# A two-layer encoder step on one core: five hand-overs between its stages rearranged, the differential map combined ahead of the next maxima, and the values of a step ahead of the second part of a weight block

## The reference

```python
hn = rms_norm(h, norm_mix_g)
z = hn @ w_in        # split into qa, ka, va, cq, dkv, ga, gb
oa = diff_attention(qa, k_all, v_all, q_pos, k_pos, lam, bias_table)   # 8 heads, two maps each
oa = rms_norm(oa, a_subln_g) * (1.0 - lam_init) @ w_a_br
ob = mla_attention(...) @ w_b_br                                       # 8 heads, latent keys
m = sigmoid(ga) * oa + sigmoid(gb) * ob
h = h + m @ w_out
h = h + conv_ffn(rms_norm(h, norm_ffn_g))
```

## Time and profile before

| | |
|---|---|
| median of 3 runs | 3051.67 us (3051.27 to 3070.66) |
| profiled execution | 3043.57 us, of which the span of instructions is 3042.0 |
| PE busy | 2723.2 us, 90% of the span |
| PE weight loads | 2505.8 us, 82% (they overlap the products) |
| DVE, ACT, POOL busy | 1467.0, 941.2, 252.0 us |
| mean granted TensorE clock | 0.939 of full speed |
| differential loops | 614.5 to 814.4 and 2100.0 to 2299.6 us |

### The profile page before, as it was taken

How to read it: one execution, slowest core, us unless ns; L and a number is a source line. 1 busy time by engine, 2 the same in 40 slices (tenths; PEclk the granted TensorE clock), 3 DMA queues, 4 the chain that set the end, 5 groups by cost and what they waited for, 6 DMA issues and landing times.

```text
span 3042.0 us, 53054 instructions
## 1 busy us (share of the span) xinstructions
PE 2723.2 (90%) x17464; PEld 2505.8 (82%) x17464; DVE 1467.0 (48%) x2602; ACT 941.2 (31%) x2032; POOL 252.0 (8%) x684
## 2 busy tenths in 40 slices
PE   5898989789889899999988889997997999999996
PEld 5875879667689899999978568885776988999996
DVE  5635221244444674655657342213445347646375
ACT  3324223345421331322233332233453113323122
POOL 3100100110000010100001011011000001001010
PEclk8979989889999999999989899998999999999998
DMA  4220114411122222222123002234111222222222
GB/s 124 52 60 0 51 44 124 149 44 42 39 62 63 67 69 73 73 69 74 58 65 70 27 8 64 68 116 134 42 39 42 76 63 66 69 73 73 69 69 75
DMA packets 376797, 201.32 MB, mean 66 GB/s; under 512 B 66438, under 2 KB 368636, under 8 KB 376658
## 3 DMA queue, kind: packets, MB, share of 16 engines
q1 hardware_dynamic: 346722, 178.99, 21.0%
q10 hardware_dynamic: 25344, 12.27, 1.3%
q0 software_dynamic: 4592, 8.35, 0.9%
HBM read 183.84 MB, written 17.88 MB: 66 GB/s over the span
## 4 chain that ended last, share of the span: by engine, by line
PE 77%; DVE 6%; issue 6%; ACT 4%; DVEq 3%; DMA 2%; ACTq 1%; SPq 0%; POOL 0%; POOLq 0%
PE ps L547 21%; PE ps L551 20%; PE ps L548 20%; PE ps L687 1%; PE ps L644 1%; PE ps L714 1%; DVE rstd L1638 1%; DMA k_past<-in_cache_a_k 1%; ACT w_hi L1171 1%; PE ps L586 1%; PE ps L589 1%; PE ps L617 1%; PE ps L712 1%; DVEq L1749 1%; PE tp L702 1%
## 5 line engine op out<-in xcount | busy, mean ns | idle before, releaser
L547 PE MATMUL ps<-hn_hi,w_hi 128*128 128x328 f32 x2848 | 893.0, 320 | 13.7 <-DVE ob_lo L1937 7.7
L548 PE MATMUL ps<-hn_lo,w_hi 128*128 128x328 f32 x2848 | 878.3, 314 | 0.0
L551 PE MATMUL ps<-hn_hi,w_lo 128*128 128x328 f32 x2848 | 662.8, 315 | 0.0
L1620 DVE TENSOR_TENSOR w_lo<-w_raw,w_hi 128x1024 fp32r<-128x1024 f32 x300 | 366.9, 1223 | 511.4 <-ACT w_hi L1171 505.6
L1171 ACT ACTIVATE w_hi<-w_raw 128x1024 fp32r<-128x1024 f32 x300 | 316.7, 1057 | 849.0 <-PE ps L551 627.6
L547 PEld LDWEIGHTS ps<-hn_hi,w_hi 128*128 128x128 f32 x2848 | 539.1, 189 | 34.7 <-issue 29.8
L548 PEld LDWEIGHTS ps<-hn_lo,w_hi 128*128 128x128 f32 x2848 | 539.7, 190 | 0.2
L551 PEld LDWEIGHTS ps<-hn_hi,w_lo 128*128 128x128 f32 x2848 | 485.8, 189 | 0.0
L547 PE MATMUL ps<-s_hi,w_hi 128*128 128x328 f32 x704 | 220.7, 320 | 18.5 <-DVE w_lo L1620 14.0
L548 PE MATMUL ps<-s_lo,w_hi 128*128 128x328 f32 x704 | 220.3, 318 | 0.0
L551 PE MATMUL ps<-s_hi,w_lo 128*128 128x328 f32 x704 | 166.9, 320 | 0.0
(11 more groups left out here) (333 smaller groups left out, 4130.7 us busy)
## 6 DMA issues: line engine op xcount, KB each, us to landing
w_raw<-in_w_in SPq DMA_DIRECT2D x98, 512.0 KB
w_raw<-in_w_up SPq DMA_DIRECT2D x88, 512.0 KB
w_raw<-in_w_down SPq DMA_DIRECT2D x32, 512.0 KB
out<-tok_out ACTq DMA_DIRECT2D x32, 256.0 KB, 2.3
k_past<-in_cache_a_k SPq DMA_DIRECT2D x16, 512.0 KB, 5.0
v_past<-in_cache_a_v SPq DMA_DIRECT2D x16, 512.0 KB, 3.5
w_raw<-in_w_a_br SPq DMA_DIRECT2D x16, 512.0 KB
w_raw<-in_w_out SPq DMA_DIRECT2D x16, 512.0 KB
```

The lines of the kernel that those rows point to most:

```text
L547: mm(dst[:, c, :], w_hi[:, slot, k, :], x_hi[:, k, cols], start=(k == 0), stop=False)
L548: mm(dst[:, c, :], w_hi[:, slot, k, :], x_lo[:, k, cols], start=False, stop=False)
L551: last = mm(dst[:, c, :], w_lo[:, slot, k, :], x_hi[:, k, cols], start=False, stop=(k == nk - 1))
L1620: tt(w_lo[:, slot], w_raw[:, slot], w_hi[:, slot].bitcast(F32), ALU.subtract).then_inc(w_split[slot], 1)
```

## The change

Nothing is computed differently. In the order of the layer:

- Latent outputs: the eight products of the first key block stand between the eight heads' small products, ahead of the wait for ob_done.
- Decode part: SP loads the keys of stream n+3 ahead of the values of stream n, where it was n+2.
- Before the differential loop: POOL waits only for the last decode scores and the map of the last stream but one, stages the first two heads and starts their bias loads, and then loads v_meta. PE waits for v_meta in the first `values` of two heads. In SBUF d_eT and d_bias change places, so that what is staged early lies on buffers that are free by then.
- In the loop: PE runs values(u) ahead of the second part of the block; DVE runs finish(u) and the split ahead of maxima(u+1); ACT runs the gate's tanh ahead of the exponentials.
- Behind the loop: all four first gate blocks run before the wait for on_done, then four projections, then pairs as before. DVE's splits of blocks B_MA+2, +3 and +4 stand around its reciprocal, and a buffer gate_next holds the third and fourth gates.
- Output projection: the first block begins when six mixed tiles are ready, and waits for the seventh and eighth at its seventh and eighth products.

```diff
 o_sq, = run(names["par_rows"][0], ("o_sq", [P, 2, P]))
-ds_, d_bias, d_qs, d_eT, d_ks = run(
-    ZW, ("d_s", [P, 2, 2, PM]), ("d_bias", [P, 2, PM]), ("d_qs", [P, 2, SEQ]),
-    ("d_eT", [P, 2, QT + 1, P]), ("d_ks", [P, 2, PM]))
+ds_, d_eT, d_qs, d_bias, d_ks = run(
+    ZW, ("d_s", [P, 2, 2, PM]), ("d_eT", [P, 2, QT + 1, P]), ("d_qs", [P, 2, SEQ]),
+    ("d_bias", [P, 2, PM]), ("d_ks", [P, 2, PM]))
 o_stage, = run(names["d_qs"][0], ("o_stage", [P, 2, SEQ]))
...
 m_lo, = run(ZW, ("m_lo", [P, KD, T], F32R))
-gate, mixed = run(names["v_tok"][0], ("gate", [P, 2, T]), ("mixed", [P, 2, T]))
-assert names["mixed"][1] <= names["v_tok"][1]
+gate, mixed, gate_next = run(names["v_tok"][0], ("gate", [P, 2, T]), ("mixed", [P, 2, T]), ("gate_next", [P, 2, T]))
+assert names["gate_next"][1] <= names["v_tok"][1]
...
+        def first_a_block(t, n):
+            src = (w_in_v[l][:, :, COL_GA + t * P:COL_GA + (t + 1) * P], a_br_v[l][:, :, t * P:(t + 1) * P])[n]
+            load(l, B_MA + 4 * n + t, 0, KD, src)
         b_block(0, 0, 0)
...
         past_keys_after(3)
+        past_keys_after(4)
         for n in range(2, STREAMS):
-            if n + 2 < STREAMS:
-                past_keys_after(n + 2)
+            if n + 3 < STREAMS:
+                past_keys_after(n + 3)
             past_values(n)
...
                 b_block(i, *divmod(jn, 2))
-        with e.Fori(0, KD // 2) as i:
+        for n in range(2):
+            for t in range(4):
+                first_a_block(t, n)
+        with e.Fori(2, KD // 2) as i:
             for jn in range(4):
...
             step = l * H * QT + i2 * 2 * QT + u
+            if u == 0:
+                e.wait_ge(v_meta_loaded, l * 16 + 16)
             e.wait_ge(a["pT"], step + 1)
...
                     scores(*then)
+                values(i2, u)
                 mix_part(i2, u, 1)
-                values(i2, u)
...
+        slot = block_ready(l, B_K, 0)
         for h in range(H):
...
             last.then_inc(olat_mm, 1)
+            last = product(slot, h, KD, hn_hi, hn_lo)
+        last.then_inc(block_done[slot], 1)
...
-        for j in range(2):
-            project(l, B_K + j, 0, KD, hn_hi, hn_lo)
+        project(l, B_K + 1, 0, KD, hn_hi, hn_lo)
         tile_turned(0, 0)
...
         e.wait_ge(dn["out_done"], (l + 1) * OUTPUTS)
-        e.wait_ge(v_meta_loaded, l * 16 + 16)
         e.sem_inc(past_wait, 1)
...
                     outputs_turned(h)
+        for t in range(2, 4):
+            project(l, B_MA + t, 0, KD, hn_hi, hn_lo)
         e.wait_ge(on_done, l + 1)
...
-        for j in range(2):
-            project(l, B_MA + 2 + j, 0, KD, oa_hi, oa_lo)
-        with e.Fori(1, KD // 2) as i:
+        for t in range(4):
+            project(l, B_MA + 4 + t, 0, KD, oa_hi, oa_lo)
+        with e.Fori(2, KD // 2) as i:
             for n in range(2):
...
                     project(l, B_MA + 2 * n + j, i * 2, KD, *((hn_hi, hn_lo), (oa_hi, oa_lo))[n])
-        e.wait_ge(m_done, l * KD + KD)
-        e.sem_inc(past_wait, 1)
-        job(l, B_OUT, KD // 2, KD, m_hi, m_lo)
+        slot = block_ready(l, B_OUT, 0)
+        for k in range(KD):
+            if k == 0 or k >= KD - 2:
+                e.wait_ge(m_done, l * KD + max(k + 1, KD - 2))
+                e.sem_inc(past_wait, 1)
+            last = product(slot, k, KD, m_hi, m_lo)
+        last.then_inc(block_done[slot], 1)
+        project(l, B_OUT + 1, 0, KD, m_hi, m_lo)
+        job(l, B_OUT, KD // 2, KD, m_hi, m_lo, first=1)
...
             for u in range(2 * QT):
+                if u % 4 == 2:
+                    gate_b(i2, u // 4)
                 then = step_after(i2, u, 1, final)
...
                     exps(*then)
-                if u % 4 == 2:
-                    gate_b(i2, u // 4)
                 transposed(i2, u)
...
             s = arrived(l, B_MA + j, i * 2)
-            e.wait_ge(gate_used, l * KD if isinstance(i, int) else l * KD + t - 1)
+            e.wait_ge(gate_used, l * KD + t - 1)
             e.sem_inc(past_wait, 1)
...
+        def first_gate_a(t):
+            s = arrived(l, B_MA + t)
+            e.wait_ge(gate_used, l * KD)
+            e.sem_inc(past_wait, 1)
+            act(halves((gate, gate_next)[t // 2][:, t % 2]), accs(s), ACT.Tanh, scale=0.5).then_inc(acc_free[s], 1)
+            e.drain().then_inc(gate_ready, 1)
         for h in range(H):
...
             if h == 5:
-                gate_a(0, 0)
                 split(l, B_MA + 2)
+                first_gate_a(0)
+        split(l, B_MA + 3)
+        first_gate_a(1)
+        split(l, B_MA + 4)
+        first_gate_a(2)
         e.wait_ge(on_scaled, l + 1)
...
         act(oa_hi[:, :, 0:META], on_t[:, :, P:], ACT.Copy, scale=sub_gain).then_inc(on_hi_done, 1)
-        gate_a(0, 1)
-        split(l, B_MA + 3)
-        split(l, B_MA + 4)
-        with e.Fori(1, KD // 2) as i:
+        split(l, B_MA + 5)
+        first_gate_a(3)
+        for t in range(6, 9):
+            split(l, B_MA + t)
+        with e.Fori(2, KD // 2) as i:
             for n in range(4):
...
                 then = step_after(i2, u, 1, final)
-                if then:
-                    maxima(*then)
+                finish(i2, u)
                 if u % 2:
...
                     gated_b(i2, 0)
-                finish(i2, u)
                 e.drain()
+                if then:
+                    maxima(*then)
             gated_b(i2, 1)
...
         low_part(H - 1)
+        split(l, B_MA + 2)
         e.wait_ge(on_rms, l + 1)
...
         e.drain()
+        split(l, B_MA + 3)
         tt(on_t[:], oT_new[:], on_rstd[:], ALU.mult).then_inc(on_scaled, 1)
-        split(l, B_MA + 2)
+        split(l, B_MA + 4)
         e.wait_ge(on_hi_done, l + 1)
...
+        def gated(t, j, s, g, b, hi, lo):
+            e.wait_ge(gate_ready, l * (2 * KD) + t + (KD + 1))
+            e.sem_inc(past_wait, 1)
+            stt(halves(mixed[:, j]), halves(g), 1.0, accs(s), ALU.add, ALU.mult).then_inc(acc_free[s], 1)
+            e.drain().then_inc(gate_used, 1)
+            tt(mixed[:, j], mixed[:, j], b, ALU.add)
+            e.drain()
+            ts(hi, mixed[:, j], 0.5, None, ALU.mult)
+            e.drain()
+            stt(lo, mixed[:, j], 0.5, hi.bitcast(F32), ALU.mult, ALU.subtract).then_inc(m_done, 1)
         def mixed_tile(i, j):
             t = i * 2 + j
-            e.wait_ge(gate_ready, l * (2 * KD) + t + (KD + 1))
             s = arrived(l, B_MA + 2 + j, i * 2)
-            stt(halves(mixed[:, j]), halves(gate[:, j]), 1.0, accs(s), ALU.add, ALU.mult).then_inc(acc_free[s], 1)
-            e.drain().then_inc(gate_used, 1)
-            tt(mixed[:, j], mixed[:, j], one(mixed_b[:, ds(t, 1), :]), ALU.add)
-            e.drain()
-            ts(one(m_hi[:, ds(t, 1), :]), mixed[:, j], 0.5, None, ALU.mult)
-            e.drain()
-            stt(one(m_lo[:, ds(t, 1), :]), mixed[:, j], 0.5, one(m_hi[:, ds(t, 1), :]).bitcast(F32), ALU.mult, ALU.subtract).then_inc(m_done, 1)
-        for j in range(2):
-            split(l, B_MA + 3 + j)
-            mixed_tile(0, j)
-        with e.Fori(1, KD // 2) as i:
+            gated(t, j, s, gate[:, j], one(mixed_b[:, ds(t, 1), :]), one(m_hi[:, ds(t, 1), :]), one(m_lo[:, ds(t, 1), :]))
+        split(l, B_MA + 5)
+        for t in range(4):
+            if t < 3:
+                split(l, B_MA + 6 + t)
+            s = arrived(l, B_MA + 4 + t)
+            gated(t, t % 2, s, (gate, gate_next)[t // 2][:, t % 2], mixed_b[:, t], m_hi[:, t], m_lo[:, t])
+        with e.Fori(2, KD // 2) as i:
             for n in range(4):
...
-    def stage_heads(kind, l, rows, src, dst, biased):
+    def stage_heads(kind, l, rows, src, dst, biased, then=None):
...
         stage_pair(0, True)
+        if then:
+            then()
         with e.Fori(1, H // 2) as i2:
...
         staged_new(l * (STREAMS + 1) + STREAMS, slice(0, META), False)
-        e.wait_ge(dn["out_done"], (l + 1) * OUTPUTS)
-        for j in range(2):
-            e.wait_ge(tok_stored[j], l * (48 * KD) + 48 * KD)
+        e.wait_ge(dn["scores"], (l + 1) * (STREAMS + 1))
+        e.wait_ge(dn["pturned"], l * (STREAMS + 1) + STREAMS)
         e.sem_inc(past_wait, 1)
         e.drain()
-        e.dma_start(v_meta[:], a_v_prompt[l, 0, 0:META].rearrange("t h e -> t (h e)")).then_inc(v_meta_loaded, 16)
-        stage_heads("diff", l, slice(0, P), qT, d_qs, True)
+        def meta_values():
+            e.wait_ge(dn["pturned"], (l + 1) * (STREAMS + 1))
+            e.wait_ge(dn["out"], (l + 1) * STREAMS)
+            for j in range(2):
+                e.wait_ge(tok_stored[j], l * (48 * KD) + 48 * KD)
+            e.sem_inc(past_wait, 1)
+            e.dma_start(v_meta[:], a_v_prompt[l, 0, 0:META].rearrange("t h e -> t (h e)")).then_inc(v_meta_loaded, 16)
+        stage_heads("diff", l, slice(0, P), qT, d_qs, True, meta_values)
```

## The result

The changed kernel takes 3045.97 us in the median of 18 runs (3033.11 to 3055.14), the kernel before on the same chip 3055.89 us (18 runs, 3045.36 to 3070.66). The ratio is 0.9962 with a 95% interval of 0.9948 to 0.9977: a gain of 11.6 us where 28 were forecast, and 2 us above the upper end of the range. Of the 22 us between 3024 and 3046 some 4 are the base, which gave 3055.89 here and 3051.67 in the runs shown before. The rest, 18 us by the medians and 16 by the ratio, is the subject of what follows. The prediction took 30 us for the least that a measurement can tell; with 18 runs a side the interval is 4 to 5 us each way.

The account below looks back on a forecast made before the run. PE, busy 2723 of 3042 us, was taken as the bound. Joints gaining 63 us and a loop costing 35 gave -28: 3014 from the profiled span, 3024 as median, range 3004 to 3044.

Parts of the forecast that it names:

- The joints: PE's waits outside the steady differential loop, which the change was to shorten or remove; claimed gain 63 us in all.
- oa_lo and m_lo: PE's waits for the differential outputs' low part and, before the output projection, the mixed map; gains 22 and 14 us.
- v_meta, first maxima and past keys: At the differential loop's start, PE's waits for v_meta and DVE's first maxima, gain 11 us; waits for past keys, 6.
- The joint of ob_lo: Latent outputs: key block products between the heads start the second key block 6 us sooner; gain 5 per layer, 10 in all.
- ends about 14 us after 411.4: Latent outputs: the eight heads and the first key block's eight products, interleaved, were to end about 14 us after their start.
- The loop: Reorderings in the differential loop: cost 35 us, between 25 and 45, with 5.0 us idle per head for 2.44 before.
- The terms for the gate, the projection and the third step's values: PE's waits per head of the differential loop: ACT's gate 1.1 us, projection out of d_acc 1.5, one step's values 1.0.
- Maxima come later: Differential loop: DVE's later maxima cost nothing, because the next scores and exponentials have a block's whole first part ahead.
- Clock falls in the loop: Rival, chance 0.16: PE's clock falls six to twelve times in the differential loop, about 1.5 us each; 3033 to 3042 us.
- The cover isn't missed: Rival, chance 0.12: waits for values and d_acc overlap, so the differential loop costs 10 us; time about 3000.
- Slower than before: Rival, chance 0.06: clock falls at nearly all 32 hand-overs of d_acc add 48 to 54 us; 3072 to 3078.
- A joint that doesn't mend: Rival, chance 0.08: behind the differential loop, B_MA+3's split or the scaling comes late, losing 3 to 4 us per layer; 3031.

Follow-up runs that it names:

- the last two kernels: Changed kernel with values behind the second part and VectorE's split behind the maxima, without and with ScalarE's outputs ahead of exponentials: 2959.12 us and 2956.94 us.

## Why the prediction was wrong, by its own steps

**The joints: 63 forecast, 59 measured (51 to 67), 55 by stretches.** oa_lo and m_lo were to give 36; the stretches they lie in gave 15.9 + 15.5 + 2.4 + 2.3 = 36.1. The wait for w_lo ahead of B_MA+3 came, and its size is right. From the timeline of the kernel after:

```profile
861.22 0.39 PE L555 MATMUL ps<-hn_hi,w_hi 128*128 128x328 f32 x1 [1.13 <-DVE w_lo L1651]
```

v_meta, first maxima and past keys were to give 17, and gave 7.2 + 3.5 + 2.8 + 2.3 = 15.8. The joint of ob_lo is the mis-sized one: 10 forecast, 3.1 by the stretches and 4.3 by undoing it. The step "ends about 14 us after 411.4" failed: heads and products together took 15.8 us (the granted clock was 0.50 from 404.3 to 418.0), and then the idle tail of 2.6 us and the second low stretch came as forecast and ate 1.7 of the 3.8 that were left.

**The loop: 35 forecast, 47 measured.** The terms for the gate, the projection and the third step's values were right to 0.1 us, and so was the vanished wait for d_s. The step that failed is one clause: "Maxima come later, but the next scores and exponentials have a whole first part of a block ahead of them: nothing". It counted what stands ahead of the scores on PE, and not what had been put ahead of the maxima on DVE: a split that itself waits for ACT, a drain and a bias fill. With only the split moved away a head falls from 27.4 to 26.2, so this clause holds 1.2 us a head: 15.6 us by the loops' windows, 23 by the ratios. Either is more than the 12 by which the loop exceeded its forecast, because the rest of the sum was too high: 35, where the loop without the split in that place costs 31 by the windows and 25 by the ratios. The waits were not what was too high (5.19 us of idle time in a head against 5.0), but PE's busy time was: the forecast kept the 21.66 us of the head before, and the heads shown with the values early at full clock have 20.8 to 21.1. The runs don't show where this difference of 0.5 to 0.8 us comes from. Here two errors of opposite sign met, and by luck the miss of the total is smaller than the forgotten term. The prediction had even named the split as the thing queued ahead of the map before, and priced its removal (1.3), but not its new place.

**The sum.** 12 us of the loop and 4 of the joints make the 16 us between -28 and -11.6. By the ratios that holds by construction, since the loop's 47 is the difference of two of them; the profiles, which measure the loop by itself, give 11 and 8.

**The rivals.** *Clock falls in the loop*: in the changed kernel's profile it stays at 1.00 up to the last head of a layer (824.2 in layer 0, 2305.6 in layer 1). The last head takes 27.5 us in layer 0 and 29.4 in layer 1, so a few microseconds of the miss may be of this kind, but not the bulk of it. It was a real danger all the same: ten falls in the two loops with the gate behind, twelve with finish first and values late, one in every second head with the maxima first. The Trainium skill's "TensorE: Matmul & The Clock Gate", section "A second HAM failure mode: psum-queue depth-cycling", describes a kernel whose clock swings between its two levels as PE idles briefly between groups of matmuls. The windows of the run with the maxima first agree that the clock swings in such a loop, with 0.94 and 28.2 us against 1.00 and 26.2; that the short idles are the cause isn't shown here. *The cover isn't missed*: out, the values' old place is worth 58 us with the new maps. *Slower than before*: not here. The values alone are slower than before, at 1.0132, but mostly by their waits: the clock falls six times in its two loops, which at 2.0 us each is 12 of its 40. *A joint that doesn't mend*: not the one named (B_MA+3), but ob_lo by over half.

## What to carry to other kernels

When an operation is moved ahead in a queue, the price list needs a line for everything that is now behind it, and for what those operations wait for: a split that waits for another engine belongs behind whatever is ready before it. An operation that covers the hand-over of a single buffer should be moved only together with a new cover; here moving the same values costs 3 us in the steps without a hand-over and 55 in the steps with one. And orders on different engines have to be priced together: with the values late, combining the map first costs 30 us if the gate is late and nothing in the loop if it is first.

## What was not expected of the hardware

Less waiting can bring no time. With the maxima first a head at full clock is 1.1 us shorter than in the changed kernel, and yet the clock falls to 0.50 (1.2 GHz) in every second head. Windows of that kernel around one fall (the 3.4 us ahead of it and the fall):

```profile
655.90:659.30 3.40, 2.05 (x14) 1.22 (x12) 0.70 (x1) 1.33 (x5) 0.00 (x0) 1.00 0.62 153
659.30:662.70 3.40, 3.40 (x16) 3.29 (x14) 0.00 (x0) 0.71 (x3) 0.00 (x0) 0.50 0.03 6
```

Ahead of the fall PE had holes of 0.45 and 0.90 us within three microseconds; the changed kernel has 0.31 and 1.48 in the same place [its timeline above] and doesn't fall. Why one pattern trips it and the other doesn't stays open. What a fall costs is plain: 2.0 us in the head that has it (28.21 for 26.23 with the maxima first, 27.12 for 25.08 with the finish first and the gate late). One more limit showed in the other direction: with nothing to wait for, a head of 21.57 us at granted clock 1.00 has PE busy for 21.46 by the profile, so in the loop of the last two kernels waits have nothing left to give.
